# The first modulation of a two-block transformer: four chunks of the contraction in four column groups of TensorE, half of it behind the first products

## What is computed

```
sc, scc = silu(c), silu(c_ctx)
for li in range(2):
    m  = split(sc  @ ada_w[li] + ada_b[li], 9)      # ada_w: 1024 x 9216
    mc = split(scc @ ada_w[li] + ada_b[li], 9)
    h  = half_ffn(h,  norm_g[li, 0], m[0],  m[1],  m[2],  ffn_w_gu[li, 0], ffn_w_down[li, 0])
    hc = half_ffn(hc, norm_g[li, 0], mc[0], mc[1], mc[2], ffn_w_gu[li, 0], ffn_w_down[li, 0])
    ...
norm_mod(h, g, shift, scale) = rms_norm(h, g) * (1 + scale) + shift
```

## Time and profile before

| | us |
|---|---|
| median of 3 runs | 3400.24 |
| lowest and highest run | 3397.33, 3403.83 |
| span of the profiled execution | 3398.0 |
| first product of the first feed-forward in it (L669) | 41.89 |
| third weight tile's first product in it | 62.01 |

### The profile page before, as it was taken

How to read it: one execution, slowest core, us unless ns; L and a number is a source line. 1 busy time by engine, 2 the same in 40 slices (tenths; PEclk the granted TensorE clock), 3 DMA queues, 4 the chain that set the end, 5 groups by cost and what they waited for, 6 DMA issues and landing times. The chain is left out here.

```text
span 3398.0 us, 46483 instructions
## 1 busy us (share of the span) xinstructions
PE 3301.7 (97%) x18292; PEld 3053.0 (90%) x18292; DVE 2275.5 (67%) x3841; ACT 1235.4 (36%) x2071; POOL 80.7 (2%) x190
## 2 busy tenths in 40 slices
PE   8999999999999999989999999989999999999999
PEld 6999999988899999989999999977888888888777
DVE  5979896467677777787777766664333766466654
ACT  5111112256553433363433343543222432334432
POOL 0000000000000000000000000000000000000100
PEclk9999999999999999999999999999999999999999
DMA  5545553200132222232232221112233320122232
GB/s 209 186 168 180 191 176 110 73 26 26 42 88 67 87 87 79 90 84 65 73 100 87 93 87 61 44 61 87 94 100 95 124 63 20 54 78 74 69 100 94
DMA packets 95272, 313.57 MB, mean 92 GB/s; under 512 B 11424, under 2 KB 15712, under 8 KB 93520
## 3 DMA queue, kind: packets, MB, share of 16 engines
q1 hardware_dynamic: 88128, 290.04, 25.9%
q0 software_dynamic: 6928, 20.55, 2.2%
HBM read 300.06 MB, written 4.19 MB: 90 GB/s over the span
## 5 line engine op out<-in xcount | busy, mean ns | idle before, releaser
L669 PE MATMUL psum<-zh,wh 128*128 128x384 f32 (+2 forms) x2384 | 777.1, 371 | 24.3 <-DVE h L752 5.7
L639 ACT ACTIVATE wh<-raw 128x512 fp32r<-128x512 f32 (+3 forms) x551 | 447.4, 817 | 836.3 <-PE psum L669 431.9
L669 PE MATMUL psum<-zh,rawl 128*128 128x384 f32 (+2 forms) x2384 | 750.9, 360 | 0.0
L669 PE MATMUL psum<-zl,wh 128*128 128x384 f32 (+2 forms) x2372 | 747.6, 360 | 0.0
L649 DVE TENSOR_TENSOR rawl<-raw,wh 128x512 fp32r<-128x512 f32 (+3 forms) x551 | 502.6, 927 | 242.9 <-ACT wh L639 241.6
L669 PEld LDWEIGHTS psum<-zh,wh 128*128 128x128 f32 x2384 | 439.5, 190 | 79.5 <-issue 25.5
L1135 PE MATMUL psum<-formq,wh 128*128 128x386 f32 x1848 | 479.7, 341 | 10.9 <-DVE made_l L649 4.1
L669 PEld LDWEIGHTS psum<-zh,rawl 128*128 128x128 f32 x2384 | 441.2, 190 | 43.0
L669 PEld LDWEIGHTS psum<-zl,wh 128*128 128x128 f32 x2372 | 438.9, 190 | 41.5 <-issue 2.9
L1135 PEld LDWEIGHTS psum<-formq,wh 128*128 128x128 f32 x1848 | 337.5, 189 | 16.5 <-DVE made_l L649 5.0
L752 DVE SCALAR_TENSOR_TENSOR h<-psum,mod,h 128x512 f32<-128x512 f32 (+1 forms) x288 | 170.0, 627 | 190.7 <-PE psum L669 190.6
(11 more groups left out here) (494 smaller groups left out, 4747.7 us busy)
## 6 DMA issues: line engine op xcount, KB each, us to landing
raw<-in_wup SPq DMA_DIRECT2D x176, 512.0 KB, 4.1
modw<-in_mod_w SPq DMA_DIRECT2D x128, 512.0 KB, 3.7
raw<-in_w_sw SPq DMA_DIRECT2D x36, 512.0 KB, 3.6
raw<-in_wdn SPq DMA_DIRECT2D x64, 256.0 KB, 3.9
raw<-in_wdn SPq DMA_DIRECT2D x32, 448.0 KB, 3.2
adaw<-in_ada_w SPq DMA_DIRECT2D x8, 1024.0 KB, 15.0
raw<-in_wdn SPq DMA_DIRECT2D x16, 512.0 KB, 4.0
raw<-in_od_in SPq DMA_DIRECT2D x16, 512.0 KB, 3.6
```

Of the source, the lines that this page charges most:

```text
L639: nc.scalar.activation(hi_of(n, i), x, ACT.Copy).then_inc(w_hi, 1)
L669: last = nc.tensor.matmul(psum[:, at + to:at + to + e - s], w[:, q * P:(q + 1) * P], x[:, q, s:e], start=(q == 0 and j == 0), stop=(q == s ...
```

## The change

- All ada tiles are taken in full fp32; the eight splits (`ada_hi`, `ada_lo`), `scc4` and `adawl` are gone. The first two weight tiles now start the list of splits.
- `scc` is 32 columns wide: the two vectors and 30 columns of zeros (a memset on VectorE). `ada_pe(h)` works on one MB: its four chunks i go to four ranges of 32 partitions of the same bank, `psum[32*i:32*i + 32]`, that is to four groups of 32 columns of the array. The second MB of a block adds to the same four ranges.
- `ada_sums` copies all 128 partitions. `ada_columns` multiplies with a matrix of two columns, `sel128[:, 20:22]`, that sums the four groups and transposes in one; the result goes to the front of the same bank, in place of a place of its own (`MT`). Block b + 2 of the accumulation therefore waits for `mod_done` rather than `ada_row`. `ada_mod` has one addition less.
- `start_pe` runs only MBs 0 to 3, with columns 0 and 1. MBs 4 to 7 stand behind chunks 0 to 3 of the first products, columns 2 behind chunk 2, and behind chunk 3 the norm sums (chunk 4 before) and then columns 3.
- On ScalarE and VectorE the order is: sums and modulation 0 and 1, operand 0, the splits of the two weight tiles, operands 1 to 3, sums and modulation 2 and 3, operands 4 to 7.

```diff
-        scc = sb("scc", ZQ_AT + words(256), [KD, 4])
-        scc4 = sb("scc4", ZQ_AT + words(320), [KD, 4], f32r)
+        scc = sb("scc", ZQ_AT + words(256), [KD, 32])
...
-        adawl = sb("adawl", R_AT, [12, 1024], f32r)
...
-        NSUM, MT, ADA_ACC, MOD_AT = 3072, 2816, 3072, 3072
+        NSUM, ADA_ACC, MOD_AT = 3072, 3072, 3072
...
         def norm_factors(dve, k):
             dve.wait_ge(n_r, k + 1)
-        SUMS_BEHIND = {0: 4, 1: 2, 2: 3, 3: 2, 4: 3, 6: 3}
+        SUMS_BEHIND = {0: 3, 1: 2, 2: 3, 3: 2, 4: 3, 6: 3}
         def beside_first(pe, k):
             return dict(ready=lambda q: pe.wait_ge(n_z, OPERAND_SPLITS[k] + q + 1),
                         side=lambda q: beside(pe, k, q))
         def beside(pe, k, q):
-            if k == 0 and q == 0:
-                ada_columns(pe, 3)
+            if k == 0 and q < 4:
+                ada_pe(pe, q + 4)
+            if k == 0 and q == 2:
+                ada_columns(pe, 2)
             if q == SUMS_BEHIND[k]:
                 norm_sums(pe, k)
+            if k == 0 and q == 3:
+                ada_columns(pe, 3)
         def norm_pe(pe, k, tokens):
...
-        ada_row, ada_tr, scc_hi, scc_lo, silu_c = [S(x) for x in
-            ("ada_row", "ada_tr", "silu_c_hi", "silu_c_lo", "silu_c")]
+        ada_row, ada_tr, scc_zero, silu_c = [S(x) for x in ("ada_row", "ada_tr", "silu_c_zero", "silu_c")]
...
                 ins = nc.vector.tensor_scalar(m, m, 0.5, None, ALU.mult)
             ins.then_inc(mod_done, 1)
-        def ada_pe(pe, j):
-
-
-            b = j // 4
+        def ada_pe(pe, h):
+
+
+            b = h // 2
             at = ADA_ACC + b % 2 * 512
-            if j % 4 == 0 and b >= 2:
-                pe.wait_ge(ada_row, b - 1)
-            if j % 2:
-                pe.wait_ge(w_lo, SPLIT_NO[j, 0])
-            else:
-                pe.wait_ge(ada_in[j // 2], 16)
-            for c in range(2):
-                k, part = j % 4 * 2 + c, slice(c * 512, (c + 1) * 512)
-                if j % 2 == 0:
-                    last = nc.tensor.matmul(psum[0:4, at:at + 512], scc[:, k, :], adaw[:, j % 12, part],
-                                            start=(k == 0), stop=False)
-                else:
-                    for i, w in enumerate((hi_of(j), adawl[:, j % 12, :])):
-                        last = nc.tensor.matmul(psum[0:4, at:at + 512], scc4[:, k, :], w[:, part],
-                                                start=False, stop=(k == 7 and i == 1))
-            last.then_inc(tile_done, 1)
+            if h % 2 == 0 and b >= 2:
+                pe.wait_ge(mod_done, b - 1)
+            pe.wait_ge(ada_in[h], 16)
+            for i in range(4):
+                j, c = 2 * h + i // 2, i % 2
+                last = nc.tensor.matmul(psum[32 * i:32 * i + 32, at:at + 512], scc[:, 4 * (h % 2) + i, :],
+                                        adaw[:, j % 12, c * 512:(c + 1) * 512], start=h % 2 == 0, stop=h % 2 == 1)
+                if c:
+                    last.then_inc(tile_done, 1)
         def ada_columns(pe, b):
             pe.wait_ge(ada_row, b + 1)
             for i in range(4):
-                m = MT + b % 4 * 16 + i * 4
-                last = nc.tensor.transpose(psum[:, m:m + 4], adarow[0:4, b % 2, i * P:(i + 1) * P], ident[0:4, 0:4])
+                m = ADA_ACC + b % 2 * 512 + i * 2
+                last = nc.tensor.matmul(psum[:, m:m + 2], adarow[:, b % 2, i * P:(i + 1) * P], sel128[:, 20:22],
+                                        start=True, stop=True)
             last.then_inc(ada_tr, 1)
-
-        def ada_hi(act, h):
-            n = 2 * h + 1
-            act.wait_ge(ada_in[h], 16)
-            if HI_WAIT[n, 0]:
-                act.wait_ge(tile_done, HI_WAIT[n, 0])
-            nc.scalar.activation(hi_of(n), adaw[:, n % 12, :], ACT.Copy).then_inc(w_hi, 1)
-
-        def ada_lo(dve, h):
-            n = 2 * h + 1
-            dve.wait_ge(w_hi, h + 1)
-            nc.vector.tensor_tensor(adawl[:, n % 12, :], adaw[:, n % 12, :], hi_of(n),
-                                    ALU.subtract).then_inc(w_lo, 1)
         def ada_sums(act, b):
             act.wait_ge(tile_done, 4 * b + 4)
             if b >= 2:
                 act.wait_ge(ada_tr, b - 1)
             at = ADA_ACC + b % 2 * 512
-            nc.scalar.activation(adarow[0:4, b % 2, :], psum[0:4, at:at + 512], ACT.Copy).then_inc(ada_row, 1)
+            nc.scalar.activation(adarow[:, b % 2, :], psum[:, at:at + 512], ACT.Copy).then_inc(ada_row, 1)
         def ada_mod(dve, b):
             layer, col = ADA_ORDER[b]
             kind, c = col // 2, slice(4 * (col % 2), 4 * (col % 2) + 4)
             dve.wait_ge(ada_tr, b + 1)
             m = mod[:, layer, kind, c, :]
-            both = psum[:, MT + b % 4 * 16:MT + b % 4 * 16 + 16].rearrange("p (c n) -> p c n", n=4)
-            link(dve, "dve", nc.vector.tensor_tensor(
-                m, both[:, :, 0:2], bc(adab[:, layer, kind * KD + c.start:kind * KD + c.stop], [P, 4, 2]), ALU.add))
-            mod_finish(dve, layer, kind, c, 2, nc.vector.tensor_tensor(m, m, both[:, :, 2:4], ALU.add))
+            at = ADA_ACC + b % 2 * 512
+            both = psum[:, at:at + 8].rearrange("p (c n) -> p c n", n=2)
+            mod_finish(dve, layer, kind, c, 2, nc.vector.tensor_tensor(
+                m, both, bc(adab[:, layer, kind * KD + c.start:kind * KD + c.stop], [P, 4, 2]), ALU.add))
         def start_sp(sp):
             for dst, src in first_loads:
...
                     last = nc.tensor.transpose(psum[:, a % 2 * 1024 + c * P:a % 2 * 1024 + (c + 1) * P],
                                                xin[:, a, c * P:(c + 1) * P], ident[:])
                 last.then_inc(x_tr, 1)
-            pe.wait_ge(scc_lo, 1)
-            for j in range(ADA_START):
-                ada_pe(pe, j)
-                if j % 4 == 1 and j >= 4:
-                    ada_columns(pe, j // 4 - 1)
+            pe.wait_ge(scc_zero, 1)
+            pe.wait_ge(silu_c, 1)
             wait_consts(pe)
+            for h in range(4):
+                ada_pe(pe, h)
+                if h >= 2:
+                    ada_columns(pe, h - 2)
             for s in x_cp:
                 pe.wait_ge(s, 3)
...
         def start_act(act):
             act.wait_ge(first_in, 16 * len(first_loads))
             nc.scalar.activation(scc[:, :, 0:2], csc[:], ACT.Silu).then_inc(silu_c, 1)
-            act.wait_ge(silu_c, 1)
-            nc.scalar.activation(scc4[:, :, 0:2], scc[:, :, 0:2], ACT.Copy).then_inc(scc_hi, 1)
             for a in (0, 2, 4):
                 act.wait_ge(x_in[a // 2], 16)
                 if a:
...
                 nc.scalar.activation(xsq[:, 0, :], xin[:, a, :], ACT.Square, accum_out=ssx[:, a:a + 1]).then_inc(x_sq, 1)
                 act.wait_ge(x_tr, a + 1)
                 nc.scalar.activation(*x_copy(a), ACT.Copy).then_inc(x_cp[0], 1)
-            for h in range(4):
-                ada_hi(act, h)
-                if h == 2:
-                    ada_sums(act, 0)
+            ada_sums(act, 0)
+            ada_sums(act, 1)
             act.wait_ge(x_cp[0], 3)
             act.wait_ge(x_cp[1], 3)
-            ada_hi(act, 4)
-            ada_sums(act, 1)
-            ada_hi(act, 5)
             operand_hi(act, 0, 0)
-            operand_hi(act, 0, 1)
-            ada_hi(act, 6)
+            split_hi(act, ADA_START)
+            split_hi(act, ADA_START + 1)
+            for c in range(1, 4):
+                operand_hi(act, 0, c)
             ada_sums(act, 2)
-            operand_hi(act, 0, 2)
-            ada_hi(act, 7)
-            split_hi(act, ADA_START)
-            operand_hi(act, 0, 3)
-            split_hi(act, ADA_START + 1)
             ada_sums(act, 3)
             for c in range(4, KD):
                 operand_hi(act, 0, c)
...
                 dve.wait_ge(x_tr, a + 1)
                 nc.vector.tensor_copy(*x_copy(a)).then_inc(x_cp[1], 1)
             wait_consts(dve)
-            for h in range(4):
-                ada_lo(dve, h)
             ada_mod(dve, 0)
-            ada_lo(dve, 4)
-            ada_lo(dve, 5)
             ada_mod(dve, 1)
             operand_lo(dve, 0, 0, scale)
-            operand_lo(dve, 0, 1, scale)
-            ada_lo(dve, 6)
-            operand_lo(dve, 0, 2, scale)
-            ada_lo(dve, 7)
+            split_lo(dve, ADA_START)
+            split_lo(dve, ADA_START + 1)
+            for c in range(1, 4):
+                operand_lo(dve, 0, c, scale)
             ada_mod(dve, 2)
-            split_lo(dve, ADA_START)
-            operand_lo(dve, 0, 3, scale)
-            split_lo(dve, ADA_START + 1)
             ada_mod(dve, 3)
             for c in range(4, KD):
                 operand_lo(dve, 0, c, scale)
...
-    c["c_sel128"] = np.repeat((x == 18).astype(f), P, 0)
+    c["c_sel128"] = ((x == 18) | (x == 20 + i[:, None] % 32) & (x < 22)).astype(f)
```

(12 more changed lines are left out.)

## The result

The changed kernel takes 3405.01 us (median of 15 runs, 3401.24 to 3412.40), the kernel before 3399.71 us on the same chip (15 runs, 3397.12 to 3404.28). The ratio is 1.0017, with a 95% interval of 1.0010 to 1.0024: about 5.3 us slower, inside the 0.2% that the prediction called hard to tell from no change, though the interval lies above 1. The forecast was 3404.9. The sum came out, but not by its own steps: it had the cost of a set and the clock wrong and left out a line of the diff, and by luck these cancelled.

A forecast was written before the change was run, and what follows sets the result against it. PE, busy for 97% of the span, was taken to bound the kernel. Third tile at 65.2 us plus 1.5 for the clock gave 66.7 against 62.01, 4.7 later; on 3400.24 that made 3404.9 us, range 3396 to 3416.

The forecast's parts named there:

- The change touches only work before the third weight tile: Whole kernel: only the third tile's start on PE matters, 62.01 us before, 66.7 forecast.
- Handed on unchanged to all that follows: After the first 62 us: PE works 537.99 of 538 us to 600, so time gained or lost there stays.
- It would be wrong if PE idled anew after 70 us: Sign against the forecast: new idle time on PE later than 70 us, behind the opening.
- A set costs 2.15 us, a staircase: Opening, one MB's four matmuls on PE: neighbouring groups half overlap, five steps of 0.43 us; chance 0.48.
- rival A: Opening's sets: all four column groups overlap fully, 0.95 us a set, third tile at 58.5, total 3398.2 us; chance 0.27.
- Columns at 1.0 us: Opening on PE: a block's columns, eight records of full-precision matmuls, take 1.0 us against 0.40 for the transposes replaced.
- The change of operands, 0.1 us a set: Sets behind the first products' chunks on PE: 0.1 us added for the operand change, 2.25 us each.
- First products at 31.3 by the staircase, 29.5 by A: Opening: PE's first products start at 31.3 us, or 29.5 with full overlap of the groups, against 41.89 before.
- The new wait ahead of chunk 4, 2.8 us, and ScalarE's chain, factors 11.9 us after columns 3: First pair of tiles: PE idles 2.8 us for columns 3; ScalarE's norm factors come 11.9 us after them.
- That the second low clock falls into ScalarE's wait: Ahead of the third tile: low clock after chunk 4's idle falls into PE's 1.85 us wait, costing up to 1.0 more.
- The clock, 1.5 us once, between 0 and 2.9: Opening: half clock after PE's 4 us idle ahead of the first products, charged 1.5 us, ends 0 and 2.9.
- Rival C: Opening's sets: the groups don't overlap, 3.45 us a set, third tile at 75.1, total 3414.8 us; chance 0.20.

The follow-up runs named there:

- e3_warm: The changed kernel with PE's idle gaps in the opening filled with identity products that nobody reads; 3400.22 us, 1.0002 of the kernel before.
- c2_after: The changed kernel run and profiled once more, with nothing altered; 3408.17 us, 1.0022 of the kernel before.
- e2_one_group: The changed kernel with all four chunks of a set added up in one column group; 3424.05 us, 1.0067 of the kernel before.
- b2_reorder_all: The changed kernel with MBs 4 to 7 reordered behind the products, c rows later on ScalarE, gaps filled, ring start back at 8; 3394.68 us, 0.9982 of before.
- e6_ring: The changed kernel with the ring of places for high halves started at 8 again, not 0; 3403.33 us, 1.0006 of the kernel before.

## Why the prediction was right, and where it was wrong

The forecast was +4.7 us and the profile shows +5.2. That the two are so near is luck, as the steps show:

- **"The change touches only work before the third weight tile".** Wrong. I took the line with `q` for the removal of eight entries of a list, and did not follow what else is counted from it. It costs 3.2 us at 957 us, in every kernel here that has another count than 8. "It would be wrong if PE idled anew after 70 us", the prediction said, and that came about. "Handed on unchanged to all that follows" was right of the opening's time (893.3 us from T3 to the pair for a T3 of 59.45, 61.97 and 64.73). But the row behind "none in which something else holds it" ends at 600 us; from 950 to 1000 us PE is busy for 45.3 of 50 us in the kernel before.
- **A set costs 2.15 us, a staircase.** Wrong: 1.00 to the next start, and 0.86 where another set follows. The step that failed is the one from "PE starts its matmuls in program order" to "second half of group 0 beside first half of group 1". The two records of one matmul in one group don't hold back the next group's first: the four first records start within 0.02 us, and 0.43 us ahead of every second one. The lower end, which I had kept for rival A, was right. The Trainium skill, "TensorE: Matmul & The Clock Gate", section "Measured speedup vs the span model", gives the span of one matmul and a few nanoseconds per tile; the rows agree with it, 1.06 us a set against 1.02 for one matmul, and I had rated it below my reading of the rows.
- **Columns at 1.0 us** was about right (0.91, from 43.69 to 44.60 in the changed kernel). **The change of operands, 0.1 us a set**, was too little: in e3_warm a set follows the product ahead of it by 0.45 instead of 0.35, the next product follows the set's start by 0.99 instead of the 0.86 of two sets in a row, and that product takes 0.46 instead of 0.35, so that a set between chunks costs 1.2 us in all. The Trainium skill, "TensorEngine Tiling (Array Packing)", section "Key Properties", speaks of a drain at a change of tiling; in these rows each change costs some 0.1 us.
- **First products at 31.3 by the staircase, 29.5 by A.** With the clock at 1.00 they start at 29.81, 0.3 behind A, and each of the four sets behind them costs 0.15 more than A had; that is the 0.9 by which T3 in e3_warm, 59.45, is behind A's 58.5. The 32.01 of the changed kernel is the low clock and 0.45 of later landing, not the staircase.
- **The new wait ahead of chunk 4, 2.8 us, and ScalarE's chain, factors 11.9 us after columns 3.** Both right to 0.1: the idle is 2.89 (0.33 in e3_warm, where the fills take its place), and columns 3 end at 53.17 - 2.89 = 50.28 and Exp 11.9 later, as ScalarE's timeline in the changed kernel shows:

```profile
50.83 4.14 ACT L856 ACTIVATE zh<-h,amul 128x512 fp32r<-128x512 f32 x8
...
61.34 0.85 ACT L1018 ACTIVATE rf<-rf 128x768 f32<-128x768 f32 x1
```

- **That the second low clock falls into ScalarE's wait** was nearly right: PE waits 0.22 us ahead of the third tile there, and 1.50 in e3_warm, where the clock is full. The loss was just larger than the wait: VectorE's read of tile 0 starts at 62.43, released by PE, 0.2 after the factors (61.34 + 0.85 = 62.19), so PE and not ScalarE sets the end there.
- **The clock, 1.5 us once, between 0 and 2.9.** The size was too small: 1.8, some 3.7 (4.15 with the landing) and 5.3 us in three profiles of the same opening against the filled one. The place was right in one of them: in c2_after the clock falls in the idle of 4.2 us ahead of the first products, as I had it. In the two others it fell before, at 22.3 and 20.6 us, between the sets, where I had charged nothing. I had sized it by a stretch of 3.9 us of work behind one idle; here it lasted 6.8 to 17.1 us.

So the terms were: T3 without the clock 59.45 instead of 65.2 (-5.75), the clock, with the later landing, 4.15 instead of 1.5 (+2.65), together 63.60 instead of 66.7, 3.1 us too high. The ring's 3.2 us, which I had left out, made up for that, and 0.4 is what the other stretches differ by (+1.55 and -1.2 in the table at the top). The time lies in the range and within the 0.2% that I gave 0.66, but of the mechanisms I gave the wrong one the highest chance: rival A's (0.27) was the true one, and its time, 3398.2, was missed because of the clock and of the line not read. Rival C is excluded by e2_one_group.

## What to carry to other kernels

Count every edit of a diff as a change until its readers are known: an index from which a planner deals out buffers cost 3.2 us here, more than half of what the whole change cost, and 900 us away from the work that the change is about. Work that is made shorter in front of a wait leaves TensorE sparse, and what follows may run at half clock; it pays to look at the granted clock of the stretch in more than one profile, and to fill such gaps or to keep the sparse part where it waits for transfers anyway. When work is moved behind other work, follow its last result to the end: here the columns of the last block came late, and with them both PE's chunk 4 and ScalarE's chain.

## What the runs showed of the hardware

Four full-precision matmuls in four column groups, of two records each, take as long as one: two sets in a row in b2_reorder_all take 1.92 us where one takes 1.06, a pitch of 0.86 for a set, which is two records of 0.43. In one group a set has a pitch of 3.43 (three take 10.49, one 3.62), 4.0 times as long. Between products of another kind it is 1.00 against 3.55. I had expected the two records to hold up the others.

The granted clock fell to 0.50 in an opening in which PE was busy 5.2 of 8 us (14 to 22 us of the changed kernel), without an idle of more than 1.42 us, and it stayed there for 13.7 us (6.8 in c2_after, 17.1 in e6_ring); in the kernel before, with PE busy 23.60 of 26.15 us, and in the filled kernels it did not fall in the opening. It came at a different time in each execution, so the same opening differs by up to 3.5 us from one profile to the next (T3 of 61.27, 63.60 and 64.73).
